# Turned expert rows stored in another order, and the row copies of the second expert table spread over other stages

## Chip, core and metric

One NeuronCore of a Trainium2 chip runs the whole program in one launch. The metric is the device time of an execution in microseconds (us); three executions of the kernel before give 5221.38, 5224.12 and 5229.09 us, and the median, 5224.12, is the time before.

## What is computed

One layer of a bidirectional encoder on 528 positions (16 learned ones and 512 tokens) of width 2048, in float32:

```
h += W_o( sigmoid(g_A) * mLSTM_bidir(RMSNorm(h)) + sigmoid(g_B) * ConformerConv(RMSNorm(h)) )
h += PEER(RMSNorm(h))
out = RMSNorm(h)[16:]

PEER, for a token t, 8 heads:
  scores against 2 x 128 sub-keys, top 16 of each, top 16 of the 256 sums -> 16 experts (i, j) per head
  z     = <expert_u[128 i + j], t>              # first table, 16384 rows of 2048
  act   = softmax(top scores) * gelu(z)
  out_t = sum over the 128 chosen experts of act * expert_v[128 i + j]    # second table
```

The expert tables hold 128 MB each. The kernel handles 384 of the 512 tokens densely: it multiplies them with every row of both tables on TensorE. For the last 128 tokens it gathers the chosen rows (128 per token) out of HBM and does the sums on VectorE.

## The kernel before

**Stages.** All matrix products go through the same pipeline of weight blocks of 1 MB (128 x 2048 float32). Block n is loaded by a DMA from the SP queue into `w_raw` (two buffers), ScalarE rounds it into `w_hi` (L1047), VectorE makes the rest `w_lo = w_raw - w_hi` (`lo`, L1424), and TensorE does three products for one (L757 to L759), 48 matmuls over 512 columns or 96 over 264 (`blk`). `w_hi` and `w_lo` have two buffers each, so the high part of block n+2 can only be made when TensorE is through with block n. The blocks run in one numbered order: 48 for the 8 mLSTM heads (6 each), 64 for the convolution's 16 channel tiles (4 each), 16 each for `w_mo` (the first of the four square projections), `w_co`, `w_o` and `w_q` (the queries), then 128 blocks of the first expert table (dense) and 128 of the second. In the convolution VectorE also does 31 taps a channel tile, and in the queries stage the top-16 searches.

**The turned table.** The first expert table arrives in the layout that the dense product needs. The gathers need whole rows, so beside the stages heads to queries the kernel makes a second copy of the table, `u_rows`, one step for each of the 128 values of j (`m` in the code). A step: a load of 1 MB from `u_blocks` into one of two `u_raw` buffers (`u_load`, L396), a stream transpose of 32 x 32 blocks on VectorE into the single buffer `u_turned` (`u_turn`, L1431), and four stores of 256 KB from it to `u_rows` (`u_turned`, L402). VectorE waits ahead of a transpose for the four stores of the step before (`u_stored`, four semaphores `ur_st`). 38 steps lie in the heads (6 a head from the second head on), 61 in the convolution (4 a channel tile), 15 beside `w_co` and 14 beside `w_o` and the first blocks of `w_q`. In a step, SP issues the load of a weight block, waits for the transpose, issues the four stores and the next `u_load`, and then the row copies, if any.

**The row copies.** The second table is copied as well, HBM to HBM, by 128 copies of 1 MB (`row_copy`, L389) in runs of 1 KB (256 floats), all on the SP queue: 64 with the first 54 blocks, 32 in the `w_mo` stage (two a block), 32 in the queries stage (two a block). None lies in the convolution after its first blocks. Only the gathers at the very end read them.

**The gathers.** `u_row` (POOL, L687) gathers 128 rows of 8 KB by the indices ZI, which VectorE computes once (L1910 to L1918) from the chosen i and j, just ahead of the one-hot tables on which TensorE's next products wait.

Of the kernel before, what the change touches and what calls it, by code (L numbers as in the profile page):

```python
# [33 lines left out]
F32 = mybir.dt.float32  # L34
F32R = mybir.dt.float32r
U32 = mybir.dt.uint32
ALU = mybir.AluOpType
# [4 lines left out]
P = 128  # L42
D = 2048
KT = D // P
# [7 lines left out]
KEYS = 128  # L52
# [19 lines left out]
VSLOT = 3  # L72
V_FIRST, V_LAST = 1, 119
QD = P // 32
# [15 lines left out]
def encoder_block(nc, xT, w_proj, w_gate, b_gate, w_mo, w_co, w_o, w_q, u_blocks, v_blocks, cols,  # L90
# [5 lines left out]
    z_dram = nc.dram_tensor("z_scratch", (NB_E, P, NT), F32, kind="Internal").ap()  # L96
    g_dram = nc.dram_tensor("g_scratch", (NT // CH, P, KEYS * CH), F32, kind="Internal").ap()
    v_rows = nc.dram_tensor("v_rows", (KEYS // GJ, P, GJ, GJ, 256), F32, kind="Internal").ap()
    u_rows = nc.dram_tensor("u_rows", (KEYS, QD, 32, QD, KT * 32), F32, kind="Internal").ap()

    at = [(nc.sbuf_base + 31) // 32 * 32]

# [118 lines left out]
    GB, UG = [GB0, GB1], [UG0, UG1, UG2]  # L221
# [17 lines left out]
    with ExitStack() as ctx:  # L239
# [5 lines left out]
        def sem(name):  # L245
            return ctx.enter_context(nc.semaphore(name))
# [81 lines left out]
        ur_st = [sem(f"u_rows_stored{b}") for b in range(QD)]  # L328
# [39 lines left out]
        def _(sp):  # L368
# [17 lines left out]
            def row_copy(n):  # L386
                jg, d = n // GJ, n % GJ
                src = v_blocks[n, :, :].rearrange("i (j c) -> i j c", j=GJ)
                sp.dma_start(v_rows[jg, :, :, d, :], src).then_inc(vr_st, 16)  # L389

            def weights(src, n, b0):
                sp.wait_ge(w_lo, b0 + n + 1)
                sp.dma_start(RAW[n % 2][:, :], src[n]).then_inc(w_loaded[n % 2], 16)

            def u_load(m, bufs):
                sp.dma_start(bufs[0][m % 2][:, :], u_blocks[m]).then_inc(ur_ld[m % 2], 16)  # L396

            def u_turned(m, bufs, end):

                sp.wait_ge(ur_turn, m + 1)  # L400
                for b in range(QD):
                    sp.dma_start(u_rows[m, b, :, :, :].rearrange("r a n -> a r n"), bufs[1][:, b * D // QD:(b + 1) * D // QD]  # L402
                                 ).then_inc(ur_st[b], 16)
                if m + 2 < end:
                    u_load(m + 2, bufs)

            for n in range(2, NB_A1 + NB_A2):
                weights(w_proj, n, A1)
                x = n - 2
                if x == U_A1_X - 1:  # L410
                    sp.wait_ge(x_lo, KT)
                    sp.wait_ge(g_rdy, 1)
                    for v in range(2):
                        u_load(U_A1 + v, u_a1)
                if U_A1_X <= x < U_A1_X + U_A2 - U_A1:
                    u_turned(x - U_A1_X + U_A1, u_a1, U_A2)
                if x == U_A2_X - 1:
                    sp.wait_ge(hs_done, 2 * NH)
                    for v in range(2):
                        u_load(U_A2 + v, u_a2)  # L420
                if U_A2_X <= x:
                    u_turned(x - U_A2_X + U_A2, u_a2, U_B2)
                if n < 8:
                    row_copy(2 * n - 4)
                    row_copy(2 * n - 3)
                elif n < 46:
                    row_copy(n + 4)
                elif n < 52:
                    row_copy(2 * n - 42)
                    row_copy(2 * n - 41)  # L430
                elif n < 54:
                    row_copy(n + 10)
            sp.wait_ge(hs_done, 2 * NH)
            sp.dma_start(sk[:], sub_keys).then_inc(sk_ld, 16)
            for n in range(NB_16):
                weights(w_mo, n, B1)
                x = B1 + n - 2
                if x < U_A2_X + U_B2 - U_A2:
                    u_turned(x - U_A2_X + U_A2, u_a2, U_B2)
                for v in range(2):  # L440
                    row_copy(64 + 2 * n + v)
            for b0, src in ((B2, w_co), (C1, w_o)):
                for n in range(NB_16):
                    weights(src, n, b0)
# [13 lines left out]
            for n in range(NB_16):  # L458
                weights(w_q, n, Q1)
                x = Q1 + n - 2  # L460
                if x < U_C1_X + KEYS - U_C1:
                    u_turned(x - U_C1_X + U_C1, u_c1, KEYS)
                for v in range(2):
                    row_copy(96 + 2 * n + v)

            def z_load(n):
                for u in range(2):
# [55 lines left out]
        def _(pool):  # L523
# [160 lines left out]

            def u_row(p):

                pool.indirect_dma_start(UG[p % VSLOT][:, :], None, u_rows.rearrange("j b r a n -> (j b r) (a n)"),  # L687
                                        bass.IndirectOffsetOnAxis(ap=ZI[:, p:p + 1], axis=0)).then_inc(ug_ld[p % VSLOT], 16)

            def z_stores(n):  # L690
# [9 lines left out]
            for p in range(VSLOT):  # L700
                u_row(p)
            for n in range(Z_LOOK, NB_E):
                z_stores(n)
                for p in dots(n):
                    if p + VSLOT < P:
                        pool.wait_ge(ug_dot, p + 1)
                        u_row(p + VSLOT)
                if n == Z_LOOK + Z_GATE + 1:
                    for s in range(2):
                        pool.wait_ge(g_st[s], 8 * (NT // CH) + 16)  # L710
                        pool.wait_ge(z_st[s], 8 * (Z_LOOK + Z_GATE))
                    group_load(pool, 0, 0, zg_first, gg_first)
# [678 lines left out]
        def _(dve):  # L1391
# [6 lines left out]
            def step(ins):  # L1398

                ins.then_inc(v_step, 1)  # L1400
                chain["k"] += 1
                return here()

            def link(ins):

                dve.wait_ge(v_step, step(ins))
# [33 lines left out]
            for m2 in range(KT // 2):  # L1440
                a, b = ((sq0, sq1), (sq2, sq3))[m2 % 2]
# [467 lines left out]
            ei, ej = EI[:, TG, :], EJ[:, TG, :]  # L1909
            link(dve.tensor_copy(ixu[:, :], ej))  # L1910
            link(dve.tensor_scalar(ixs[:, :], ixu[:, :], 3, None, ALU.logical_shift_right))
            link(dve.tensor_copy(ixf[:, :], ixs[:, :]))
            link(dve.scalar_tensor_tensor(ixz[:, :], ej, float(P), ei, ALU.mult, ALU.add))
            link(dve.scalar_tensor_tensor(ixf[:, :], ixf[:, :], float(P * GJ - GJ), ej, ALU.mult, ALU.add))
            link(dve.scalar_tensor_tensor(ixf[:, :], ei, float(GJ), ixf[:, :], ALU.mult, ALU.add))
            dve.tensor_copy(ZI[:, :], ixz[:, :]).then_inc(ix_rdy, 1)
            dve.tensor_copy(VI[:, :], ixf[:, :]).then_inc(ix_rdy, 1)
            dve.tensor_copy(GS[:, :], GA[:, TG, :]).then_inc(ix_rdy, 1)  # L1918
# [13 lines left out]
            with dve.Fori(0, NT // CH // 2) as cc:  # L1932
                for b in range(8):
                    n = 8 * cc + b
# [12 lines left out]
            with dve.Fori(0, 8) as i:  # L1947
                for b in range(6):
                    n = 6 * i + (Z_LOOK + Z_GATE + b)
# [47 lines left out]
            for g in range(KEYS // GJ):  # L1997
                par, more, tail = g % 2, g < KEYS // GJ - 1, g == KEYS // GJ - 1
                for r in range(8):
                    n = 8 * g + r  # L2000
# [95 lines left out]
```

## Time and profile before

| | |
|---|---|
| median of three executions | 5224.12 us |
| the profiled execution, its time | 5226.97 us |
| its span, first to last instruction | 5225.4 us |
| TensorE busy | 4625.4 us, 89% |
| VectorE busy | 3327.7 us, 64% |
| mean granted TensorE clock | 0.945 |
| moved by DMA | 1272.96 MB |

The span is cut into stretches in what follows. A stretch's row gives the busy time of each engine with its number of instructions, then the granted clock of TensorE as a share of 2.4 GHz, the mean busy share of the 16 DMA engines and what they moved. "PE busy" counts a matmul that runs at the lower clock as busy for its longer time. A time from issue to landing runs from the DMA's instruction to its semaphore.

### The profile page before, as it was taken

How to read it: one execution, taken by the hardware profiler on the slowest of the kernel's cores; microseconds unless marked ns; L12 is line 12 of the kernel's file. 1: busy time of each engine (PE TensorE's matmuls, PEld its weight loads, DVE VectorE, ACT ScalarE, POOL GpSimd, SP SyncE). 2: the span in 40 equal slices, each digit the busy share in tenths (PEclk: the TensorE clock that was granted, in tenths of full speed). 3: DMA queues.
4: the chain of work that ended last, by engine and by line, in shares of the span. 5: the costliest groups of instructions: out<-in, count | busy, mean ns of one | idle time of the engine just before them, and what ended most of it. 6: DMA issues, size and time to landing. Idle time of an engine off the chain costs nothing.

```text
span 5225.4 us, 66426 instructions
## 1 busy us (share of the span) xinstructions
PE 4625.4 (89%) x24985; PEld 4220.1 (81%) x24985; DVE 3327.7 (64%) x4044; ACT 1306.1 (25%) x1217; POOL 710.3 (14%) x742
## 2 busy tenths in 40 slices
PE   8988889867777778976769899999999999999998
PEld 6767667766666666865657799999999999999998
DVE  5555456555555565433238978887776578888886
ACT  4222222111111112311121234443222322222223
POOL 1000101000000002000001111222332011111112
PEclk9989999988888888998989999999999999999999
DMA  6666666555555558655567357778888688888884
GB/s 233 240 233 234 233 233 239 196 185 190 179 194 183 193 181 301 226 187 183 205 226 273 125 178 276 287 289 325 339 332 297 240 300 316 308 309 307 313 289 164
DMA packets 383856, 1272.96 MB, mean 244 GB/s; under 512 B 22144, under 2 KB 198160, under 8 KB 276128
## 3 DMA queue, kind: packets, MB, share of 16 engines
q1 hardware_dynamic: 329728, 940.49, 50.5%
q0 software_dynamic: 54048, 331.51, 17.3%
q8 instruction: 37, 0.61, 0.0%
q14 instruction: 43, 0.35, 0.0%
HBM read 1070.46 MB, written 335.61 MB: 269 GB/s over the span
## 4 chain that ended last, share of the span: by engine, by line
PE 47%; DMA 32%; DVE 10%; SPq 6%; issue 3%; ACT 1%; POOL 1%; DVEq 0%; POOLq 0%; ACTq 0%
DMA u_rows<-u_turned_a 23%; PE bank L757 15%; PE bank L758 15%; PE bank L759 15%; SPq L402 5%; DVE u_turned_a L1431 4%; DMA u_rows<-u_turned_b 4%; DMA u_rows<-u_turned_c 3%; PE bank L981 1%; DMA u_raw_a<-u_blocks 1%; DVE w_lo L1424 1%; DVE u_turned_b L1431 1%; POOL cand L674 1%; ACT w_hi L1047 1%; DVE u_turned_c L1431 1%
## 5 line engine op out<-in xcount | busy, mean ns | idle before, releaser
L757 PE MATMUL bank<-x_hi,w_hi 128*128 128x384 f32 (+2 forms) x5760 | 2049.1, 356 | 540.9 <-DVE w_lo L1424 424.5
L758 PE MATMUL bank<-x_lo,w_hi 128*128 128x384 f32 (+2 forms) x5760 | 2029.4, 352 | 0.0
L759 PE MATMUL bank<-x_hi,w_lo 128*128 128x384 f32 (+2 forms) x5760 | 2017.5, 350 | 0.0
L757 PEld LDWEIGHTS bank<-x_hi,w_hi 128*128 128x128 f32 x5760 | 1143.1, 198 | 679.5 <-issue 449.2
L1047 ACT ACTIVATE w_hi<-w_raw 128x2048 fp32r<-128x2048 f32 x432 | 826.8, 1914 | 2177.6 <-PE bank L759 1717.6
L1424 DVE TENSOR_TENSOR w_lo<-w_raw,w_hi 128x2048 fp32r<-128x2048 f32 x432 | 993.7, 2300 | 350.8 <-ACT w_hi L1047 348.9
L759 PEld LDWEIGHTS bank<-x_hi,w_lo 128*128 128x128 f32 x5760 | 1143.0, 198 | 88.0
L758 PEld LDWEIGHTS bank<-x_lo,w_hi 128*128 128x128 f32 x5760 | 1143.8, 199 | 86.3 <-issue 1.2
L1431 DVE STREAM_TRANSPOSE u_turned_a<-u_raw_a 128x2048 f32<-128x2048 f32 x99 | 228.8, 2311 | 767.1 <-DMA u_rows<-u_turned_a 767.1
L757 PE MATMUL bank<-x_hi_o,w_hi 128*128 128x384 f32 x2048 | 684.4, 334 | 0.6 <-DVE w_lo L1424 0.4
L759 PE MATMUL bank<-x_hi_o,w_lo 128*128 128x384 f32 x2048 | 684.1, 334 | 0.0
L758 PE MATMUL bank<-x_lo_o,w_hi 128*128 128x384 f32 x2048 | 684.1, 334 | 0.0
L757 PEld LDWEIGHTS bank<-x_hi_o,w_hi 128*128 128x128 f32 x2048 | 384.5, 188 | 1.2 <-issue 1.2
L758 PEld LDWEIGHTS bank<-x_lo_o,w_hi 128*128 128x128 f32 x2048 | 384.5, 188 | 0.0
L759 PEld LDWEIGHTS bank<-x_hi_o,w_lo 128*128 128x128 f32 x2048 | 384.5, 188 | 0.0
L1990 DVE SCALAR_TENSOR_TENSOR v_sums<-v_row,gate_pairs,v_sums 128x2048 f32<-128x2048 f32 x128 | 300.3, 2346 | 1.0
L1929 DVE SCALAR_TENSOR_TENSOR u_row<-u_row,x_rows 128x2048 f32<-128x2048 f32 x128 | 290.3, 2286 | 0.0
L716 POOL DMA_INDIRECT v_row<-v_rows,v_index x128 | 153.2, 1197 | 836.0 <-DVE v_sums L1990 832.6
L687 POOL DMA_INDIRECT u_row<-u_rows,z_index x128 | 185.8, 1452 | 345.9 <-DVE u_row L1929 333.6
L1616 DVE SCALAR_TENSOR_TENSOR r<-glu,conv_w,r 128x512 f32 (+1 forms) x240 | 178.4, 743 | 0.0
L1616 DVE SCALAR_TENSOR_TENSOR conv_odd<-glu,conv_w,conv_odd 128x512 f32<-128x512 f32 x224 | 166.5, 743 | 0.0
L1845 DVE TENSOR_TENSOR z_stage<-bank,rstd_b 128x384 f32<-128x384 f32 x128 | 71.2, 556 | 148.1 <-PE bank L759 140.0
(280 smaller groups left out, 2689.6 us busy)
## 6 DMA issues: line engine op xcount, KB each, us to landing
v_rows<-v_blocks SPq DMA_DIRECT2D x128, 1024.0 KB, 11.7
w_raw<-u_blocks SPq DMA_DIRECT2D x128, 1024.0 KB, 5.7
w_raw<-v_blocks SPq DMA_DIRECT2D x128, 1024.0 KB, 4.9
w_raw<-w_proj SPq DMA_DIRECT2D x112, 1024.0 KB, 13.7
u_raw_a<-u_blocks SPq DMA_DIRECT2D x99, 1024.0 KB, 13.6
u_rows<-u_turned_a SPq DMA_DIRECT2D x396, 256.0 KB
z_scratch<-z_stage POOLq DMA_DIRECT2D x128, 192.0 KB, 3.4
g_scratch<-g_chunk SPq DMA_DIRECT2D x12, 2048.0 KB, 12.1
```

The lines of the kernel that those rows point to most:

```text
L402: sp.dma_start(u_rows[m, b, :, :, :].rearrange("r a n -> a r n"), bufs[1][:, b * D // QD:(b + 1) * D // QD]).then_inc(ur_st[b], 16)
L687: pool.indirect_dma_start(UG[p % VSLOT][:, :], None, u_rows.rearrange("j b r a n -> (j b r) (a n)"), bass.IndirectOffsetOnAxis(ap=ZI[:, p: ...
L716: pool.indirect_dma_start(VG[p % VSLOT][:, :], None, v_rows.rearrange("g i j d c -> (g i j) (d c)"), bass.IndirectOffsetOnAxis(ap=VI[:, p: ...
L757: pe.matmul(dst, whi, xhi, start=start, stop=False)
L758: pe.matmul(dst, whi, xlo, start=False, stop=False)
L759: return pe.matmul(dst, wlo, xhi, start=False, stop=stop)
L1047: act.activation(WH[s][:, :], RAW[s][:, :], ACT.Copy).then_inc(w_hi, 1)
L1424: dve.tensor_tensor(WL[s][:, :], RAW[s][:, :], WH[s][:, :].bitcast(F32), ALU.subtract).then_inc(w_lo, 1)
L1431: dve.transpose(bufs[1][:, :].rearrange("p (b k c) -> p b k c", b=QD, c=32), bufs[0][s][:, :].rearrange("p (k b c) -> p b k c", b=QD, c=32 ...
L1616: at_.append(step(dve.scalar_tensor_tensor(acc, x, w, acc, ALU.mult, ALU.add)))
L1929: dve.scalar_tensor_tensor(UG[s][:, :], UG[s][:, :], 1.0, XR[:, :, :, :].rearrange("p a k c -> p (a k c)"), ALU.mult, ALU.mult, accum_out= ...
L1990: dve.scalar_tensor_tensor(ACC[:, :], VG[p % VSLOT][:, :], GS[:, p:p + 1], ACC[:, :], ALU.mult, ALU.add).then_inc(vg_use, 1)
```

## The change

Two things are changed, and the index arithmetic follows the first.

First, the order of `u_rows`. Before, each of the four stores of a step took 512 columns of all 128 partitions (quarter `b`) and wrote them in the order a, r, n, with a outermost (4 values, a = partition / 32). After, each store takes all 2048 columns of 32 partitions (quarter `a`) and writes them in the order r, b, n, with r outermost (32 values). Both move 256 KB in 128 runs of 2 KB. A gathered row stays 8 KB in one piece.

Second, the row copies. After, blocks 2 to 49 have one each (48), every second block from 50 to 111 has one (31, in the convolution), one follows the last, `w_mo` keeps two a block (32), and the queries have one a block (16).

```diff
-    u_rows = nc.dram_tensor("u_rows", (KEYS, QD, 32, QD, KT * 32), F32, kind="Internal").ap()
+    u_rows = nc.dram_tensor("u_rows", (KEYS, 32, QD, QD, KT * 32), F32, kind="Internal").ap()
...
-                for b in range(QD):
-                    sp.dma_start(u_rows[m, b, :, :, :].rearrange("r a n -> a r n"), bufs[1][:, b * D // QD:(b + 1) * D // QD]
-                                 ).then_inc(ur_st[b], 16)
+                for a in range(QD):
+                    sp.dma_start(u_rows[m, :, :, a, :], bufs[1][32 * a:32 * a + 32, :].rearrange("r (b n) -> r b n", b=QD)
+                                 ).then_inc(ur_st[a], 16)
...
-                if n < 8:
-                    row_copy(2 * n - 4)
-                    row_copy(2 * n - 3)
-                elif n < 46:
-                    row_copy(n + 4)
-                elif n < 52:
-                    row_copy(2 * n - 42)
-                    row_copy(2 * n - 41)
-                elif n < 54:
-                    row_copy(n + 10)
+                if n < 50:
+                    row_copy(n - 2)
+                elif n % 2 == 0:
+                    row_copy(48 + (n - 50) // 2)
             sp.wait_ge(hs_done, 2 * NH)
             sp.dma_start(sk[:], sub_keys).then_inc(sk_ld, 16)
+            row_copy(79)
...
                 for v in range(2):
-                    row_copy(64 + 2 * n + v)
+                    row_copy(80 + 2 * n + v)
...
-                for v in range(2):
-                    row_copy(96 + 2 * n + v)
+                row_copy(112 + n)
...
-                pool.indirect_dma_start(UG[p % VSLOT][:, :], None, u_rows.rearrange("j b r a n -> (j b r) (a n)"),
+                pool.indirect_dma_start(UG[p % VSLOT][:, :], None, u_rows.rearrange("j r b a n -> (j r b) (a n)"),
...
-            link(dve.scalar_tensor_tensor(ixz[:, :], ej, float(P), ei, ALU.mult, ALU.add))
+            link(dve.tensor_scalar(ixz[:, :], ei, float(QD), None, ALU.mult))
+            link(dve.scalar_tensor_tensor(ixz[:, :], ej, float(P), ixz[:, :], ALU.mult, ALU.add))
...
+            link(dve.tensor_copy(ixu[:, :], ei))
+            link(dve.tensor_scalar(ixs[:, :], ixu[:, :], 5, None, ALU.logical_shift_right))
+            link(dve.scalar_tensor_tensor(ixz[:, :], ixs[:, :], 1.0 - 32 * QD, ixz[:, :], ALU.mult, ALU.add))
```

## Rows read from the trace of the kernel before

**Rows 1.** The page: busy time by engine, and the chain that ended last, by line.

```profile
PE 4625.4 (89%) x24985; PEld 4220.1 (81%) x24985; DVE 3327.7 (64%) x4044; ACT 1306.1 (25%) x1217; POOL 710.3 (14%) x742
...
DMA u_rows<-u_turned_a 23%; PE bank L757 15%; PE bank L758 15%; PE bank L759 15%; SPq L402 5%; DVE u_turned_a L1431 4%; DMA u_rows<-u_turned_b 4%; DMA u_rows<-u_turned_c 3%; PE bank L981 1%; DMA u_raw_a<-u_blocks 1%; DVE w_lo L1424 1%; DVE u_turned_b L1431 1%; POOL cand L674 1%; ACT w_hi L1047 1%; DVE u_turned_c L1431 1%
```

**Rows 2.** Stretches: us, busy (x), PEclk, DMA share, GB/s; head one, heads, convolution.

```profile
61.00:84.00 23.00, 23.00 (x191) 1.00 0.68 232
...
84.60:172.60 88.00, 88.00 (x496) 72.00 (x495) 53.99 (x50) 23.33 (x25) 15.35 (x24) 1.00 0.68 245
...
284.70:506.50 221.80, 187.60 (x990) 152.93 (x989) 120.27 (x105) 47.91 (x50) 19.83 (x38) 0.92 0.66 236
...
1028.10:1944.80 916.70, 677.62 (x3744) 608.60 (x3744) 513.48 (x547) 127.12 (x105) 54.33 (x39) 0.86 0.53 186
```

**Rows 3.** Stretches, same columns: in `w_mo`, `w_co` and `w_o`, queries (two), dense table.

```profile
2057.00:2168.50 111.50, 111.50 (x481) 90.07 (x480) 42.98 (x37) 38.58 (x38) 23.46 (x22) 1.00 0.79 278
...
2216.00:2694.60 478.60, 361.78 (x1377) 284.26 (x1375) 159.75 (x113) 71.52 (x60) 33.97 (x42) 0.88 0.54 193
...
2694.60:2770.00 75.40, 47.66 (x193) 37.83 (x194) 35.32 (x60) 19.33 (x23) 0.56 (x1) 0.82 0.76 272
2770.00:2932.40 162.40, 151.49 (x693) 122.55 (x691) 144.48 (x624) 29.11 (x30) 26.78 (x24) 1.00 0.67 228
...
3610.00:4000.00 390.00, 388.90 (x2209) 388.58 (x2208) 281.43 (x230) 107.27 (x92) 136.11 (x118) 1.00 0.91 342
```

**Rows 4.** The chain in order of time in the convolution: start us, us, what.

```profile
1219.33 0.51 SPq L402
...
1221.10 12.18 DMA u_rows<-u_turned_a
...
1233.40 2.32 DVE u_turned_a L1431
```

**Rows 5.** Waits: convolution (DVE, PE), heads, `w_co` and `w_o`: total, times, longest us.

```profile
DVE u_turned_a L1431 <- DMA u_rows<-u_turned_a: 402.7, 52, 14.3
...
PE bank L757 <- DVE w_lo L1424: 237.4, 39, 11.0
...
DVE u_turned_a L1431 <- DMA u_rows<-u_turned_a: 200.1, 20, 13.8
...
DVE u_turned_b L1431 <- DMA u_rows<-u_turned_b: 150.7, 13, 13.0
DVE u_turned_c L1431 <- DMA u_rows<-u_turned_c: 111.5, 11, 10.7
```

**Rows 6.** DMA issues of the convolution stretch, count, KB each, median us to landing.

```profile
w_raw<-w_proj SPq DMA_DIRECT2D x52, 1024.0 KB, 11.7
...
gate_a_scratch<-gate_stage POOLq DMA_DIRECT2D x13, 256.0 KB, 7.8
gate_b_scratch<-gate_stage POOLq DMA_DIRECT2D x13, 256.0 KB, 4.8
```

**Rows 7.** DMA queues and issues of the queries stretch 2770 to 2932.4.

```profile
q1 hardware_dynamic: 25097, 37.04, 67.1%
...
v_rows<-v_blocks SPq DMA_DIRECT2D x21, 1024.0 KB, 10.1
```

**Rows 8.** VectorE groups of the convolution stretch: busy us, mean ns, idle before.

```profile
L1616 DVE SCALAR_TENSOR_TENSOR r<-glu,conv_w,r 128x512 f32 x195 | 144.9, 743 | 0.0
...
L1431 DVE STREAM_TRANSPOSE u_turned_a<-u_raw_a 128x2048 f32<-128x2048 f32 x52 | 120.2, 2311 | 402.7 <-DMA u_rows<-u_turned_a 402.7
L1424 DVE TENSOR_TENSOR w_lo<-w_raw,w_hi 128x2048 fp32r<-128x2048 f32 x52 | 118.7, 2283 | 0.0
```

**Rows 9.** VectorE in order of time: start us, us; the index arithmetic, then TensorE's wait.

```profile
3097.17 0.22 DVE L1910 CAST ix_j<-ej 128x128 uint32<-128x128 f32 x1
3097.43 0.23 DVE L1911 TENSOR_SCALAR ix_group<-ix_j 128x128 uint32<-128x128 uint32 x1
...
3098.28 0.29 DVE L1914 SCALAR_TENSOR_TENSOR ix_row<-ix_row,ej 128x128 f32<-128x128 f32 x1
...
PE bank L967 <- DVEq L1905: 4.0, 1, 4.0
```

## The prediction

> **What bounds the kernel now.** I read the views in this order. The page first: TensorE is busy for 89% of the span, but the largest entry of the chain that ended last is not TensorE, it is the landing of the stores of the turned table, 23% + 4% + 3%, with 5% for issuing them [rows 1]. So for some 30% of the span the last thing to happen is a transfer. The stretches say where. Head one, which has hardly any turned steps, takes 88.0 us at a granted clock of 1.00 with TensorE busy all the time; the next heads do the same 496 matmuls in about 111 us (221.8 us for 990) [rows 2]. The convolution stretch holds 3744 matmuls, 288 a channel tile, so 13 tiles, 70.5 us each, with TensorE busy 74% and the clock at 0.86 [rows 2]. `w_co` and `w_o`: 1377 matmuls are 28.7 blocks of 48, 16.7 us each, where `w_mo`, which has two row copies a block and no turned step in the stretch shown, runs 481 matmuls in 111.5 us, 11.13 us a block at clock 1.00 [rows 3].
>
> The waits name the cause. In the convolution VectorE stands 402.7 us ahead of 52 transposes for the stores of the step before, and TensorE in turn stands 237.4 us for `w_lo`, which is queued on VectorE behind those transposes [rows 5]. Per tile VectorE works 513.48 / 13 = 39.5 us and waits 402.7 / 13 = 31.0; the sum is 70.5, the whole tile. The chain in time shows one turn of it: three issues of about 0.5 us, 12.18 us from the last issue to the landing, 2.32 us of transpose, and again [rows 4]. The stores are the clock of every stage from head two to the first queries.
>
> **Why a store is slow.** A step's four stores move 1.05 MB, and land in about 12.2 us: 86 GB/s. The 16 DMA engines move 186 GB/s at a mean busy share of 0.53 in the same stretch, so all of them together would move 186 / 0.53 = 351 GB/s, and a quarter of them 88 [rows 2, 4]. A gate tile of the same shape (128 partitions, 2 KB each, 256 KB in all) that goes out in plain partition order lands in 4.8 to 7.8 us [rows 6], so runs of 2 KB do not explain it; the store's destination with a outermost, 4 values, is what differs. I take it that a store before runs on 4 of 16 engines, and that four in a row follow each other on the same ones. The Trainium skill (DMA: Bandwidth & Descriptors, section "Why a DMA increments its semaphore by 16 and not by 1") says a copy is split over the largest number of engines up to 16 that divides the slowest dimension of both sides: 128 against 4 gives 4 before, 32 against 32 gives 16 after. By that rule, the trace agrees: 86 GB/s against 88.
>
> **The stores after.** The same 1.05 MB over all engines is 1.05 / 351 = 3.0 us of their time in place of about 12. To it come the issues (three of 0.5 us ahead of the last) and the latency and queue of one store, for which the gate tiles are the nearest row, 4.8 to 7.8 us. From the end of a transpose to the last landing I take 8 us (before: about 14). Bounds: 6.3, with the 4.8; and 14, nothing gained.
>
> *Convolution, 61 steps = 15.25 tiles.* Three floors.
> VectorE: four transposes and four `lo` a tile (2311 and 2283 ns), taps of 0.66 us each between them [rows 8]. Of the four gaps between transposes one is short (two evacuations of about 0.45 and a `lo`, 3.1 us) and three are 8.3 us or more by 9, 11 and 12 taps and a `lo`. A landing in 8 us costs 8 - 3.1 = 4.9 us in the short one and nothing in the others: 39.5 + 4.9 = 44.4 us.
> TensorE: two blocks of 96 matmuls over 264 columns (191 in 23.0 us, so 11.56 each [rows 2]) and two of 11.13: 45.4 us, if the clock is at 1.00 as in the stretches without idle time.
> DMA: 0.53 x 70.5 = 37.4 us of engine time now. The change adds two row copies a tile. In the queries stretch, nearly all row copies, 37.04 MB cost 67.1% of 162.4 us, 109 us, so 3.1 us a copy [rows 7]. 37.4 + 6.2 = 43.6 us. The highest share that a long stretch shows is 0.91 [rows 3], so 47.9 us.
> The three are within 4 us of each other, and each waits for the others in turn (`w_raw` behind the copies in the SP queue, `lo` behind taps, the transpose behind the stores). I take the highest floor and one short-gap wait: 47.9 + 4.9 = 52.8 us, between 46 (TensorE alone) and 60. 15.25 x (70.5 - 52.8) = 270 us.
>
> *Heads, 38 steps = 6.33 heads.* TensorE's floor is head one's 88.0 us. DMA: 0.66 x 111 = 73 us, at 0.91 80 us. VectorE: 60 us of work a head, and waits that now are 200.1 us in 24 steps [rows 5], 50 a head; some 14 are left where two transposes stand close together. All under 88; a late `lo` or `kT` now and then costs 3.6 us by my estimate, a quarter of those 14. 91.6 against 111: 6.33 x 19.6 = 124 us (bounds 88 and 98).
>
> *`w_co` and `w_o`.* Per block: TensorE 11.13; DMA 0.54 x 16.7 = 9.0, at 0.91 9.9; VectorE cannot turn faster than one transpose and one landing, 2.3 + 8 = 10.3. I take 12.0, and leave the 22 us at the change of stage. 28.7 x 12.0 + 22 = 366 against 478.6: 112 us (bounds 11.3 and 13.5 a block).
>
> *Queries.* The first 193 matmuls, four blocks, take 75.4 us; later ones, bound by VectorE's searches (144.48 busy of 162.4), take 12 blocks in about 162, 13.5 each [rows 3]. Four of these are 54 us; of the 21 us between I take 15, as the stores and half of the row copies leave the queue. The rest of the stage stays.
>
> *Edits at nothing or nearly.* Row copies moved out of the first heads: TensorE is at 100% there, nothing gained; that cover is TensorE itself. The copy after the last convolution block and the unchanged two a block in `w_mo`: hidden under 11.13 us blocks with a DMA share of 0.79; without that cover a copy costs 3.1 us. The gather reads the same 8 KB pieces. Index arithmetic: four more small instructions, 0.26 to 0.33 us each with their links [rows 9], 1.1 us, and TensorE waits for VectorE there (4.0 us), so it is on the path: +1.1 us. On SP a step has 4 stores at 0.5 us, two loads and at most one copy, some 4 us of an 11 us block, so the queue does not bound. The dense stages, from 2940 us on, are untouched.
>
> **Sum.** 270 + 124 + 112 + 15 - 1 = 520 us. Span 5225.4 - 520 = 4705; the profiled execution's time lies 1.6 above its span, and the median 2.9 below that time: 4704 us.
>
> **Rivals.**
> (A) *The new store runs at half rate, and DMA becomes the bound.* Sixteen engines now read from 32 partitions at a time, where each store before read from all 128. No row shows a store from 32 partitions under load. If it halves the rate, a step costs 6.0 us of all engines: tile 43.6 + 12 = 55.6, head 73 + 18 = 91, block 12.0. With waits on top I take 57, 96 and 12.8: 206 + 95 + 89 + 12 = 402, so 4822 us; at a share of 0.91, tile 61, head 100, block 13.2, savings 145 + 70 + 78 + 10, it is 4921. For it: nothing hides a DMA share that would reach 0.95. Against it: the rate is halved only while all engines are at stores. The Trainium skill (SBUF — State Buffer, section "Door 1: The DMA port swizzle") says that 32 adjacent partitions reach 8 of the 16 ports and gives 189 GB/s for them against 328 for all; by it a step would be 5.5 us, near this rival's 6.0. No run here has shown it.
> (B) *TensorE is the bound throughout.* Tile 46, head 88.5, block 11.3: 374 + 142 + 132 + 20 = 668, so 4556 us; with half of the forecast's extras, about 4620. For it: `w_mo` and head one run at their floor with DMA shares of 0.79 and 0.68. Against it: VectorE was at 0.39 and 0.61 there, it will be at 0.85 in the convolution.
> (C) *Slower.* If the landing is not a matter of the engines' number but of writes in 2 KB runs to this table, it stays at 12 us or more, and two row copies of 3.1 us a tile stand in the convolution's queue ahead of the stores: 15.25 x 6.2 = 95 us, less 10 in the queries: 5310 us. It decides if the four stores still land later than about 13.5 us after the last issue, so that the copies' 6.2 us a tile are not paid back. Rows 6 speak against it. If the copies are hidden then, nothing changes.
>
> **Chances.** Forecast (4620 to 4790) 0.57; (A) 0.23; (B) 0.14; (C) 0.05 slower; 0.01 no change. The range takes in the forecast's own, half of (B) and more than half of (A): 4580 to 4880. Faster by over 0.2% 0.94, within 0.2% (about 10 us, what a measurement of this kernel can tell) 0.01, slower 0.05.
>
> **What would show it.** In the trace after, the last issue to landing of a step near 5 us and not 12 (the engines' number); the wait ahead of the transposes down from 402.7 us to under 100 in the convolution; TensorE's clock there at 0.95 or more; tiles near 53, heads near 92, blocks near 12 us; a DMA share of 0.8 to 0.9 in the convolution. (A) would show as waits for `w_raw` or the landing at 8 us or more with a share above 0.9. (B) as no TensorE wait for `w_lo`. Wrong altogether if the landing is as before, or if the dense stages change by more than a few us.

## The result and the profile after

The changed kernel takes 4560.84 us (median of 4; 4559.16 to 4562.37) against 5224.64 (median of 4) for the kernel before: a ratio of 0.8729, 95% interval 0.8714 to 0.8744. The forecast was 4704, its range 4580 to 4880; the measured time lies 19 us below the range. The direction and the mechanism held, the size did not: 664 us were gained in place of 520, and the time is close to that of rival (B), 4556.

Here is the page of the kernel after: busy time by engine and the chain that ended last by line. From the POOL queue's code to the index arithmetic lines are numbered six lower than before (L757 is L751, L1424 is L1418, L1431 is L1425).

```profile
PE 4459.9 (98%) x24985; PEld 4091.3 (90%) x24985; DVE 3333.3 (73%) x4048; ACT 1301.7 (29%) x1217; POOL 711.9 (16%) x742
...
PE bank L751 24%; PE bank L752 24%; PE bank L753 24%; DMA u_rows<-u_turned_a 5%; SPq L402 2%; PE bank L975 2%; DVE u_turned_a L1425 2%; DMA u_rows<-u_turned_c 2%; DVE w_lo L1418 1%; PE bank L851 1%; PE bank L858 1%; DVE u_turned_c L1425 1%; PE bank L827 1%; ACT w_hi L1041 1%; POOL cand L668 1%
```

The landing of the stores, 30% of the chain before [rows 1], is down to 7%, and the three products of TensorE stand at 72%. The span is 4558.9 us. TensorE is busy 165.5 us less for the same 24985 matmuls, and its mean granted clock went from 0.945 to 0.995: a part of the gain comes by way of the clock. The stretches that answer to [rows 2, 3] follow, with the same columns: four heads, twelve convolution tiles, blocks beside `w_co` and `w_o`, the first queries, the dense table.

```profile
262.80:614.30 351.50, 351.50 (x1978) 287.48 (x1978) 244.76 (x209) 94.56 (x100) 43.50 (x76) 1.00 0.87 298
...
865.60:1440.90 575.30, 555.91 (x3477) 500.60 (x3476) 472.22 (x505) 114.73 (x96) 49.97 (x36) 1.00 0.93 317
...
1742.30:2044.00 301.70, 301.70 (x1304) 244.61 (x1303) 157.61 (x111) 68.29 (x57) 32.97 (x41) 1.00 0.91 296
2055.00:2108.00 53.00, 50.64 (x223) 40.13 (x222) 39.16 (x86) 17.39 (x19) 0.56 (x1) 1.00 0.92 333
...
2930.00:3300.00 370.00, 368.96 (x2096) 368.64 (x2095) 266.39 (x218) 100.31 (x87) 129.86 (x111) 1.00 0.91 342
```

A head takes 351.5 / 4 = 87.9 us (about 111 before), a tile 575.3 / 12 = 47.9 (70.5), a block beside `w_co` and `w_o` 301.7 x 48 / 1304 = 11.1 (16.7). In heads and blocks TensorE is busy without a gap at a granted clock of 1.00. The dense table's share and rate, 0.91 and 342 GB/s, are as before.

The waits (total, times, longest us) answer to [rows 5]. They are those of VectorE and TensorE in the convolution, of VectorE in the heads, and of VectorE beside `w_co` and `w_o`.

```profile
DVE u_turned_a L1425 <- DMA u_rows<-u_turned_a: 101.8, 25, 5.3
...
PE bank L751 <- DVE w_lo L1418: 18.6, 21, 2.4
...
DVE u_turned_a L1425 <- DMA u_rows<-u_turned_a: 27.6, 17, 2.6
...
DVE tmp_b L1721 <- PE bank L753: 57.2, 12, 4.9
...
DVE u_turned_b L1425 <- DMA u_rows<-u_turned_b: 3.1, 1, 3.1
```

In the convolution the store waits fell from 31.0 us a tile to 8.5, and 39.4 of work plus 8.5 is the whole tile of 47.9. The 8.5 us are two waits a tile, and VectorE in order of time shows which:

```profile
1022.70 2.31 DVE L1425 STREAM_TRANSPOSE u_turned_a<-u_raw_a 128x2048 f32<-128x2048 f32 x1 [5.04 <-DMA u_rows<-u_turned_a]
1036.27 2.31 DVE L1425 STREAM_TRANSPOSE u_turned_a<-u_raw_a 128x2048 f32<-128x2048 f32 x1 [3.59 <-DMA u_rows<-u_turned_a]
```

The first wait stands behind the short gap, the second behind the gap after it. The other two transposes of the tile do not wait. Beside `w_co` and `w_o` VectorE now waits for TensorE: the roles have changed. The chain in order of time, in the same tile:

```profile
1015.95 0.75 SPq L402
1016.74 5.83 DMA u_rows<-u_turned_a
1022.70 2.32 DVE u_turned_a L1425
...
1026.27 0.67 SPq L402
1026.98 9.16 DMA u_rows<-u_turned_a
```

The last issue to the landing takes 5.83 us where it took 12.18 [rows 4], and 9.16 us in the next step. The SP queue in between shows what lay ahead of the second: the next load of a turned step, a row copy and a weight load, issued between the two groups of stores.

```profile
1018.04 1.17 SPq L396 DMA_DIRECT2D u_raw_a<-u_blocks  x1
1019.25 1.16 SPq L389 DMA_DIRECT2D v_rows<-v_blocks  x1
1020.45 1.33 SPq L393 DMA_DIRECT2D w_raw<-w_proj  x1
1025.04 2.63 SPq L402 DMA_DIRECT2D u_rows<-u_turned_a  x4
```

### The profile page after: what moved, and what is told of

It is laid out like the page before. It is cut to its first block, busy times and chain, and to the rows that moved or that the text cites. A ratio compares the mean times of both kernels' runs of the same rounds, so it can differ in the third digit from the quotient of the medians.

```text
span 4558.9 us, 66430 instructions
## 1 busy us (share of the span) xinstructions
PE 4459.9 (98%) x24985; PEld 4091.3 (90%) x24985; DVE 3333.3 (73%) x4048; ACT 1301.7 (29%) x1217; POOL 711.9 (16%) x742
## 4 chain that ended last, share of the span: by engine, by line
PE 77%; DVE 8%; DMA 8%; issue 4%; SPq 2%; ACT 1%; POOL 1%; DVEq 1%; POOLq 0%; ACTq 0%
PE bank L751 24%; PE bank L752 24%; PE bank L753 24%; DMA u_rows<-u_turned_a 5%; SPq L402 2%; PE bank L975 2%; DVE u_turned_a L1425 2%; DMA u_rows<-u_turned_c 2%; DVE w_lo L1418 1%; PE bank L851 1%; PE bank L858 1%; DVE u_turned_c L1425 1%; PE bank L827 1%; ACT w_hi L1041 1%; POOL cand L668 1%
## 5 line engine op out<-in xcount | busy, mean ns | idle before, releaser
L751 PE MATMUL bank<-x_hi,w_hi 128*128 128x384 f32 (+2 forms) x5760 | 1975.9, 343 | 50.7 <-DVE w_lo L1418 38.5
L752 PE MATMUL bank<-x_lo,w_hi 128*128 128x384 f32 (+2 forms) x5760 | 1966.1, 341 | 0.0
L753 PE MATMUL bank<-x_hi,w_lo 128*128 128x384 f32 (+2 forms) x5760 | 1957.4, 340 | 0.0
L1418 DVE TENSOR_TENSOR w_lo<-w_raw,w_hi 128x2048 fp32r<-128x2048 f32 x432 | 995.3, 2304 | 417.8 <-ACT w_hi L1041 415.6
L751 PEld LDWEIGHTS bank<-x_hi,w_hi 128*128 128x128 f32 x5760 | 1084.5, 188 | 161.2 <-issue 51.7
L752 PEld LDWEIGHTS bank<-x_lo,w_hi 128*128 128x128 f32 x5760 | 1085.3, 188 | 84.6 <-issue 2.6
L753 PEld LDWEIGHTS bank<-x_hi,w_lo 128*128 128x128 f32 x5760 | 1087.3, 189 | 82.1
L751 PE MATMUL bank<-x_hi_o,w_hi 128*128 128x384 f32 x2048 | 684.4, 334 | 0.6 <-DVE w_lo L1418 0.4
L751 PEld LDWEIGHTS bank<-x_hi_o,w_hi 128*128 128x128 f32 x2048 | 384.4, 188 | 1.2 <-issue 1.2
L1425 DVE STREAM_TRANSPOSE u_turned_a<-u_raw_a 128x2048 f32<-128x2048 f32 x99 | 228.4, 2307 | 154.8 <-DMA u_rows<-u_turned_a 154.7
L2003 DVE TENSOR_TENSOR out_sums<-bank,out_sums 128x384 f32<-128x384 f32 x256 | 130.5, 551 | 52.3 <-PE bank L753 48.0
```

The costliest lines, as they stand in the source:

```text
L751: pe.matmul(dst, whi, xhi, start=start, stop=False)
L752: pe.matmul(dst, whi, xlo, start=False, stop=False)
L753: return pe.matmul(dst, wlo, xhi, start=False, stop=stop)
L1418: dve.tensor_tensor(WL[s][:, :], RAW[s][:, :], WH[s][:, :].bitcast(F32), ALU.subtract).then_inc(w_lo, 1)
L1425: dve.transpose(bufs[1][:, :].rearrange("p (b k c) -> p b k c", b=QD, c=32), bufs[0][s][:, :].rearrange("p (k b c) -> p b k c", b=QD, c=32 ...
L2003: dve.tensor_tensor(o, o_bank[r % 2][k][:, 0:NT], o, ALU.add).then_inc(evac_v, 1)
```

## The experiments

Seven kernels follow, each one edit away from the kernel after or before. Theory M, made when the result was known, says: the old store runs on 4 of 16 engines, this is the whole gain, and the copies in the convolution cost something. In the last three experiments M also says that a tile of the kernel after is VectorE's chain, its work and its waits for stores; the rival there is that the time of the DMA engines sets the tile. The other rivals are named in each expectation.

**The order alone, the copies where they were before.** The kernel after, with

```diff
-                if n < 50:
-                    row_copy(n - 2)
-                elif n % 2 == 0:
-                    row_copy(48 + (n - 50) // 2)
+                if n < 8:
+                    row_copy(2 * n - 4)
+                    row_copy(2 * n - 3)
+                elif n < 46:
+                    row_copy(n + 4)
...
+                for v in range(2):
+                    row_copy(96 + 2 * n + v)
...
```

> The new order of the turned rows with the row copies where they were before (none in the convolution after its first blocks, two a block in the queries). Theory M (a store ran on 4 of 16 engines, and this alone is the gain; the copies in the convolution cost something): heads 88 us each, as after; a convolution tile falls from 47.9 us to TensorE's own 45.4 to 46, because the landing that the third transpose waits for has no copy ahead of it; the queries give back some 10 us; total 4525 to 4550. Rival R1 (a good part of the gain comes from spreading the copies over the stages): heads or convolution stay above the times after, total over 4600.

The kernel takes 4531.08 us (median of 4), ratio to before 0.8673 (0.8658 to 0.8687): the whole gain and 30 us more. Twelve tiles:

```profile
862.30:1408.80 546.50, 546.50 (x3449) 495.99 (x3449) 474.38 (x504) 114.76 (x96) 49.91 (x36) 1.00 0.89 288
```

TensorE is busy all the time, and a tile is 45.5 us. The spreading of the copies gave nothing; it takes 2.4 us a tile. R1 falls. The queries did not give back the 10 us that M expected: from the last transpose to the first index of the gathers it is 360 us here, 359 in the kernel after with half the copies, and 357 before. The waits of VectorE in this stretch carry the lesson for the forecast:

```profile
DVE glu L1646 <- PE bank L759: 41.5, 12, 3.5
DVE w_lo L1424 <- ACT w_hi L1047: 25.3, 24, 1.6
DVE u_turned_a L1431 <- DMA u_rows<-u_turned_a: 4.8, 10, 1.3
```

In the short gap VectorE waits for TensorE's product (3.5 us a tile, `glu`) and for `w_hi` (0.9 us of the 2.1 a tile), and in that time the stores land. Of the 4.9 us a tile that the prediction put there, at most 0.4 are still waits for stores.

**The copies alone, the old order.** The kernel before, with

```diff
+                if n < 50:
+                    row_copy(n - 2)
+                elif n % 2 == 0:
+                    row_copy(48 + (n - 50) // 2)
...
```

> The old order of the turned rows with the new places of the row copies. M: nothing is gained, and the two copies a tile stand in the convolution's queue ahead of the stores, 3.1 us each, where the landing already sets the pace: tile 73 to 77 us against 70.5, total 5250 to 5310. R1: total under 5150.

It takes 5234.07 us (one run) beside 5221.92 for before. Twelve tiles take 867.0 us, 72.3 each:

```profile
1028.30:1895.30 867.00, 622.69 (x3456) 559.01 (x3456) 474.05 (x505) 115.91 (x97) 49.72 (x36) 0.85 0.59 211
...
DVE u_turned_a L1425 <- DMA u_rows<-u_turned_a: 392.5, 48, 13.5
```

There is no gain, so R1 is out from this side too. But M missed the size: it said 5250 to 5310 us in all and 73 to 77 a tile. The loss is 1.8 us a tile, under a third of the 6.2 us that M and the prediction's rival (C) charged, and nearly all of it is in the waits for stores (371.7 us before over the same twelve tiles, 392.5 here). The share rose from 0.53 to 0.59. That most of each copy lay in time that the stores left free is argued from this, not shown.

**Eight engines.** Each store takes all 128 partitions and has an outermost destination dimension of 8. The rows land in other places of `u_rows`, so the outputs of the last 128 tokens are other numbers; the work is the same.

```diff
-                for a in range(QD):
-                    sp.dma_start(u_rows[m, :, :, a, :], bufs[1][32 * a:32 * a + 32, :].rearrange("r (b n) -> r b n", b=QD)
-                                 ).then_inc(ur_st[a], 16)
+                for b in range(QD):
+                    sp.dma_start(u_rows[m, 8 * b:8 * b + 8, :, :, :].rearrange("r b a n -> (r b a) n").rearrange("(s q) n -> q s n", q=8),
+                                 bufs[1][:, b * D // QD:(b + 1) * D // QD]).then_inc(ur_st[b], 16)
```

> As after, but each store takes 512 columns of all 128 partitions and writes them with an outermost destination dimension of 8 (before: 4; after: 32 on both sides). The rows land in other places, so the gathers read other data, and the outputs of the last 128 tokens are other numbers; the work is the same. M (the outermost dimension sets how many engines a store uses, here 8): last issue to landing about 8 to 9 us, between 5.9 and 12.2; in the convolution the transposes wait 15 to 19 us a tile and a tile takes 55 to 58 us; a block beside the second and third projection 12.5 to 13.5; heads 88 to 92; total 4720 to 4800. Rival R2 (the old order was slow for another reason, such as the place in HBM that neighbouring runs go to, and any other order cures it): total as after, 4550 to 4570, or as before.

It takes 4652.82 us (one run), between 4561 and 5224 and below what M said (4720 to 4800). Its chain in time and its stretches (heads, tiles, blocks beside `w_co` and `w_o`):

```profile
1111.34 7.66 DMA u_rows<-u_turned_a
...
1123.32 9.43 DMA u_rows<-u_turned_a
...
1137.23 6.41 DMA u_rows<-u_turned_a
```

```profile
872.60:1491.70 619.10, 569.05 (x3463) 515.01 (x3461) 473.29 (x505) 114.59 (x96) 50.03 (x36) 0.96 0.83 295
1789.00:2114.50 325.50, 312.42 (x1329) 252.18 (x1328) 156.29 (x109) 67.79 (x56) 31.67 (x40) 0.98 0.75 264
174.80:702.10 527.30, 527.30 (x2967) 431.69 (x2966) 363.97 (x314) 141.84 (x150) 65.24 (x114) 1.00 0.81 294
```

The landing goes with the outermost dimension: 12.2 us at 4; 6.4 to 7.7 at 8 without a copy just ahead, and 9.4 and more with one; 5.8 and 9.2 in the kernel after. M had said 8 to 9. The number of engines can also be read from the busy share in the first 3 to 6 us after stores are issued. The rows are those of the kernel before, of this one and of the kernel after:

```profile
1236.00:1242.00 6.00, 6.00 (x52) 6.00 (x51) 6.00 (x10) 0.00 (x0) 0.00 (x0) 1.00 0.25 83
1111.00:1114.00 3.00, 2.68 (x22) 2.46 (x21) 3.00 (x6) 0.18 (x1) 0.00 (x0) 1.00 0.48 150
1015.00:1018.00 3.00, 3.00 (x14) 2.44 (x13) 2.65 (x3) 0.00 (x0) 0.00 (x0) 1.00 0.97 359
```

A quarter, a half and nearly all of the 16 engines are busy, at 83, 150 and 359 GB/s. In the kernel before, the quarter lasts for all 6 us, although the issue of the next load starts at 1238.28. (What was left of earlier loads is in these rows too, in the kernel after above all.) R2 said that any other order would give the time of the kernel after, or that of the kernel before. This store differs from the old one only in the order of its 128 runs within the same 256 KB, and it gives neither, so R2 falls. Nor can the distance between runs be the cause: consecutive runs lie 8 KB apart in the old store and in the new one alike.

The heads do not feel the slower store: 87.9 us, TensorE at 100%. A tile is 51.6 us (M said 55 to 58) with 12.1 us of waits for stores (15 to 19), a block 325.5 x 48 / 1329 = 11.8 (12.5 to 13.5). M's number of engines is right, and its waits are too large again.

**Plain order, all engines, all partitions.** This is to price the 32 partitions from which a store of the kernel after reads. Again the rows land in other places, and the work is the same.

```diff
-                for a in range(QD):
-                    sp.dma_start(u_rows[m, :, :, a, :], bufs[1][32 * a:32 * a + 32, :].rearrange("r (b n) -> r b n", b=QD)
-                                 ).then_inc(ur_st[a], 16)
+                for b in range(QD):
+                    sp.dma_start(u_rows[m, 8 * b:8 * b + 8, :, :, :].rearrange("r b a n -> (r b a) n"), bufs[1][:, b * D // QD:(b + 1) * D // QD]
+                                 ).then_inc(ur_st[b], 16)
```

> As after, but each store takes 512 columns of all 128 partitions and writes them in plain partition order to one piece of 256 KB (again other data for the gathers and so for the last 128 tokens). It has all engines, and not the 32 partitions at a time of the new order. M without a price for 32 partitions: as after, 4550 to 4570, DMA share in the convolution 0.92 to 0.94, last issue to landing 5.9. With the half rate of 32 partitions that rival A of the prediction named: the new order spends up to 3 us more of all engines a step than this one, so here the share in the convolution falls to 0.75 or less, the landing to 4 us or less, and the tile to 45.5 us; total 4515 to 4535.

It takes 4522.27 us (one run), 39 us below the kernel after. Tiles, and blocks beside `w_co` and `w_o`:

```profile
860.60:1408.10 547.50, 547.50 (x3458) 496.97 (x3457) 473.81 (x506) 114.75 (x96) 49.91 (x36) 1.00 0.93 333
1692.90:1994.70 301.80, 301.80 (x1305) 244.66 (x1304) 156.21 (x110) 67.79 (x56) 31.68 (x40) 1.00 0.82 290
```

and the same blocks in the kernel after:

```profile
1728.90:2030.70 301.80, 301.80 (x1305) 244.66 (x1304) 156.09 (x109) 67.78 (x56) 31.66 (x40) 1.00 0.88 288
```

The total and the tile are the half-rate theory's (4515 to 4535, 45.5), the shares are not: it wanted 0.75 or less in the convolution. Beside `w_co` the new order spends (0.88 - 0.82) x 301.8 / 27.2 = 0.7 us more of the engines a step than the plain one. In the convolution it spends 0.93 x 47.9 against 0.93 x 45.6, 2.1 us a tile or 0.5 a step. The plain order differs in a second thing, the place in HBM to which neighbouring runs go, but that is not what costs: the three kernels with both copies whose stores read from 128 partitions spend 0.59 x 72.3 (old order), 0.83 x 51.6 (outermost 8) and 0.93 x 45.6 (plain), that is 42.4 to 42.8 us a tile, and the kernel after 44.6. Without copies the new order spends 0.89 x 45.5 against 0.53 x 70.5 of the old one, 3.1 us a tile or 0.8 a step. So a store from 32 partitions has a price, 0.5 to 0.8 us a step, about a fifth to a quarter of the 3.0 us of rival (A). In the landing of one store the price is larger: over six heads the median is 6.5 us in the kernel after and 3.9 here, beside `w_co` and `w_o` 5.4 to 5.7 and 4.0 to 4.2; in the convolution it is 5.9 and 6.4. Still the tile falls from 47.9 to 45.6, TensorE's own, with both copies in it. SP also issues a plain store faster, in 0.44 us (median) against 0.62; how much of the 39 us is due to that is not separated. And TensorE never waits at a DMA share of 0.93: 0.91 was no ceiling.

**One copy a tile, behind the third transpose's stores.**

```diff
-                elif n % 2 == 0:
-                    row_copy(48 + (n - 50) // 2)
+                elif n % 4 == 2:
+                    row_copy(48 + (n - 50) // 4)
...
-                row_copy(112 + n)
+                for v in range(1 if n < 4 else 3 if n >= 12 else 2):
+                    row_copy(96 + (n if n < 4 else 2 * n - 4 if n < 12 else 3 * n - 16) + v)
...
```

> The new order, with one row copy a convolution tile in place of two, issued behind the stores of the third transpose, whose followers have the longest gap (16 copies), and two, later three, a block in the queries from the fifth block on. M (a tile after is VectorE's chain, with a landing that a copy delays): the third transpose's wait of about 3.6 us a tile goes, the tile is TensorE's 45.5 to 46 us; queries as after within 5 us; total 4515 to 4535, below the kernel after (4561) and at or a little below the run with the old copies (4531). If the copies' engine time sets the tile: 46.5 to 47, total about 4545.

It takes 4528.83 us (median of 5), ratio 0.8678 (0.8665 to 0.8692), below the kernel after. Tiles:

```profile
862.10:1409.30 547.20, 547.20 (x3455) 496.68 (x3454) 474.74 (x504) 114.75 (x96) 49.90 (x36) 1.00 0.92 310
```

A tile is 45.6 us, as M said; the rival's 46.5 to 47 is out. The kernel does not differ from the one with the old places of the copies (0.8673): both are at TensorE's floor. The edit takes out a copy as well as placing the other, so it does not say which of the two did it.

**The same two copies, one block later.**

```diff
-                elif n % 2 == 0:
-                    row_copy(48 + (n - 50) // 2)
+                elif n % 2 == 1:
+                    row_copy(48 + (n - 51) // 2)
```

> As after, with the 31 copies of the convolution issued one block later, behind the stores of the second and fourth transposes of a tile. The same bytes and the same share; only the landing that each copy delays is another: the third's and the first's, and the first's is followed by the short gap. M: the waits ahead of the second transposes grow by about 3 us a tile, those ahead of the third go; the tile is 48 to 50 us, 4560 to 4590. If the share of the DMA engines sets the tile, nothing moves: 47.9 us, 4555 to 4565.

It takes 4562.04 us (one run): the time does not move, as the rival said. M's 48 to 50 us a tile and 4560 to 4590 in all hold at their lower ends only. Tiles and waits:

```profile
864.10:1439.10 575.00, 557.97 (x3493) 504.12 (x3491) 473.08 (x505) 114.75 (x96) 50.41 (x36) 0.99 0.96 317
...
DVE u_turned_a L1425 <- DMA u_rows<-u_turned_a: 100.8, 35, 6.3
```

A tile is 47.9 us. The waits spread over more transposes, 35 in place of 25, and their sum is 100.8 for 101.8. By place in the tile, the wait ahead of the third transpose fell from 3.5 us to 0.9, where M had it gone; the one behind the short gap grew from 5.0 to 5.7, where M had 3 us more; and 1.9 us stand ahead of the transpose after that third one. So a copy does delay the landing behind it, but the sum of the waits did not change with its place. The share is 0.96 for the same transfers in the same time as 0.93 in the kernel after, so a product of share and time is good to some 1.4 us a tile and no better. The price of the 32 partitions has its sign from several runs, its size is rough.

**Less VectorE work.** The last 4 of the 31 taps are done on 32 of 512 columns, so a part of the convolution is left out.

```diff
+                    if k >= 27:
+                        acc, x = acc[:, 0:32], x[:, 0:32]
```

> As after, with the last 4 of the 31 taps of the convolution done on 32 of 512 columns, so that part of the convolution is left out; some 2.4 us less of VectorE a tile, in the longest gap, and the same transfers. If VectorE's chain (work and store waits) sets the tile: 45.6 to 46 us, total about 4525 to 4535. If the DMA engines' time does (share 0.93): tile 47.5 to 48, total 4555 to 4565.

It takes 4548.41 us (one run), between the two theories. Tiles and waits:

```profile
860.40:1425.40 565.00, 553.97 (x3489) 501.37 (x3488) 451.58 (x504) 114.78 (x96) 49.95 (x36) 1.00 0.95 323
...
DVE u_turned_a L1425 <- DMA u_rows<-u_turned_a: 108.1, 36, 5.1
```

VectorE works 1.7 us less a tile (2.4 were expected), the tile is 0.9 shorter (47.1), and the store waits are 0.5 longer. Neither theory holds alone. I take it that less work lets the steps follow each other faster, and that a part comes back as later landings, with the share at 0.95; the runs fit this but do not isolate it.

## Why the prediction was wrong

*Right.* What bounds the kernel before: with the order of the stores changed, and of the rest only the index arithmetic, 690 us of 5222 go. A quarter of the engines: outermost dimensions of 4, 8 and 32 give shares of 0.25, 0.48 and 0.97 and landings of 12.2, about 7 and 5.8 us. The rule of the Trainium skill on how many engines carry a copy (DMA: Bandwidth & Descriptors, section "Why a DMA increments its semaphore by 16 and not by 1") fits all three. TensorE's floors: 88.0, 45.4 and 11.13 us forecast, 87.9, 45.5 and 11.1 measured. The clock: 1.00 where TensorE has no gaps. The engine time of a tile: 43.6 us forecast, 44.6 measured. The index arithmetic: from the first conversion to the first one-hot table VectorE takes 4.90 us after against 3.80, the 1.1 us; but TensorE's wait there is 4.0 us in both, so it was not seen to reach the path.

*Wrong: what was added to the floors.*

The step that failed first is the convolution's term, "I take the highest floor and one short-gap wait: 47.9 + 4.9 = 52.8 us". Measured are 47.9, and 15.25 x 4.9 = 75 us of the 143 that the forecast was off. The wait of 4.9 us was real: it is 5.0 us in the tile shown above. But it belongs to VectorE's chain, whose floor of 44.4 us has it already, and it was added a second time, to the floor of another engine. VectorE's chain was short of a term in its turn: "nothing in the others" is 3.5 us a tile, where the landing behind a load, a row copy and a weight load comes 11.1 us after the end of the transpose and not 8. (The wait is 0.9 us when the copy is moved away.) Its 39.4 + 5.0 + 3.5 = 47.9 us are the tile. That the DMA floor is also 47.9 is luck. It was 43.6 us at a share of at most 0.91, and the runs show 0.93 with TensorE at 100% and 0.96 otherwise; and its 3.1 us a copy came from a stretch read as "nearly all row copies", in which 21 of the 33 transfers of 1 MB are row copies and 12 are loads. With the copies out of the way, TensorE paces the tile: VectorE waits 3.5 us for the product in the short gap, and the landing is under it. Waits of one engine in the same gap overlap; each floor was worked out as if the others did not exist, and then they were added.

The blocks beside `w_co` and `w_o`, "I take 12.0, and leave the 22 us at the change of stage": measured 11.1 and no wait of TensorE in 301.7 us, 28.7 x (16.7 - 11.1) = 160 us in place of 112. The 22 us were charged as if they belonged to the stage. They were 21.4 us that TensorE waited for `x_lo`. The kernel before has this wait, and VectorE in order of time:

```profile
PE bank L757 <- DVE x_lo L1677: 21.4, 1, 21.4
...
2433.72 2.31 DVE L1431 STREAM_TRANSPOSE u_turned_b<-u_raw_b 128x2048 f32<-128x2048 f32 x1 [12.13 <-DMA u_rows<-u_turned_b]
2435.95 9.08 DVE L1677 TENSOR_TENSOR x_lo<-r,x_hi 128x512 fp32r<-128x512 f32 x15
```

VectorE stood 12.13 us for the stores just ahead of the transpose behind which it makes `x_lo`. No run isolates this wait, but it is gone in the kernel after.

SP was also priced too low, at some 4 us a step: with a copy it is 7.1 us, from the first store at 1014.71 to the end of the weight load's issue at 1021.78. In the convolution SP waits for VectorE ahead of each of the 48 groups of stores all the same, 151.3 of 575.3 us, so the queue does not hold the stores back.

The heads' 3.6 us and the queries' remainder are the third miss. Six heads (2967 matmuls) take 527.3 us where they took 658.4, so 6.33 heads gave 138 us in place of 124; the forecast had two misses there, 91.6 for 87.9 and 111 for what is 109.7 on the mean. In the queries 223 matmuls, 4.6 blocks, take 53.0 us, so four take about 46: some 30 us gained where 15 were taken. Here the margin was for "a late `lo` or `kT` now and then". The run with 8 engines shows how much slack there was: later landings, and a head is still 87.9 us. The high part of a block can be made as soon as the block before last is through, so a delay of a few us on VectorE is swallowed by an 11 us block; this reason is argued from the two buffers and not tested.

*The rivals.* (B) was right in the reason for heads and blocks. Its tile of 46 us was not reached: 47.9. Its total of 4556 is so close because this miss of 29 us is made up by blocks, where it had 132 us and 160 were gained; that is luck. (A), half rate from 32 partitions, was a fifth to a quarter true, 0.5 to 0.8 us a step of its 3.0. The Trainium skill (SBUF — State Buffer, section "Door 1: The DMA port swizzle") gives 189 GB/s for 32 partitions against 328 for all; these stores in mixed traffic show a smaller loss of engine time. (C) is refuted: the landing fell, and the copies cost 1.8 us a tile even on the slow stores. The new places of the copies cost about 30 us of what the new order gives. The prediction had them in its DMA floor only, and not in the landings behind them.

*Open.* What exactly sets the 47.9 us. The DMA engines are close to full (44.6 of 47.9 us), VectorE's work and store waits add up to the tile, and taking out either one copy (44.6 - 0.92 x 45.6 = 2.6 us of engine time) or the price of 32 partitions (2.1) brings TensorE's 45.6; shifting the copies changes nothing, less VectorE work gives half. This would fit engines so full that time won on VectorE comes back as a later landing, but no run tests it by itself. Whether a second `u_turned` buffer would bring 45.6 without taking transfers out was not tried.

## What to carry to other kernels

Compare a transfer's rate with the rate of all engines in the same stretch (moved bytes over busy share); a clean fraction, here 86 of 351 GB/s, points to the number of engines that carry it, and the busy share in the first few us after the issue (here 0.25) settles it. Then the outermost dimension of both sides is what to change. When the wait that paces a pipeline goes, make one sum for each engine, its own work and its own waits, and forecast the largest of these sums. Never add a wait of one engine to the floor of another. And price a landing by what is issued ahead of it in the queue: here it was 8 us or 11, and the second was left out. Bulk copies that nobody waits for belong where they delay no landing that a chain waits for, and not evenly everywhere: in the heads and in `w_mo` TensorE has no gap with them, in the queries half as many gained nothing, and in the convolution they cost 2.4 us a tile.

## What the runs showed of the hardware that was not expected

TensorE ran without a gap at a mean DMA share of 0.93 over 547 us (333 GB/s), and a stretch reached 0.96. The four stores of a step, each of 256 KB from 32 partitions on 16 engines, cost 0.5 to 0.8 us more engine time than four from 128 partitions, about a fifth to a quarter of the 3.0 us at 351 GB/s, and not twice as much. The landing of a single store was more than that apart: 6.5 against 3.9 us in the heads. Two row copies a tile take 4 to 5 us of every engine by the shares (0.93 x 47.9 - 0.89 x 45.5, and 0.59 x 72.3 - 0.53 x 70.5), less than the 6.2 taken from the queries stretch, where a third of the transfers were loads; they cost 1.8 us a tile when the pacing stores ran on a quarter of the engines, and 2.4 when the engines were nearly full.
